# Silu in a hybrid decoder step, written as tanh on ScalarE and a multiply-add on VectorE

## The reference

```python
def swiglu(h, w_gate, w_up, w_down):
    return (jax.nn.silu(h @ w_gate) * (h @ w_up)) @ w_down
...
def decoder_layer(x, pe, mixer, g_ffn1, w1_gate, w1_up, w1_down, g_mix, w_in, w_out,
                  g_ffn2, w2_gate, w2_up, w2_down, g_ple, w_ple_gate, w_ple_proj):
    x = x + 0.5 * swiglu(rms_norm(x, g_ffn1), w1_gate, w1_up, w1_down)
    mixed, state = mixer(rms_norm(x, g_mix) @ w_in)
    x = x + mixed @ w_out
    x = x + 0.5 * swiglu(rms_norm(x, g_ffn2), w2_gate, w2_up, w2_down)
    gate = jax.nn.sigmoid(rms_norm(x, g_ple) @ w_ple_gate)
    x = x + gate * (pe @ w_ple_proj)
    return x, state
```

## Time and profile before

| | |
|---|---|
| median of three runs | 2749.54 us (2747.8 to 2750.54) |
| profiled execution, first to last instruction | 2748.0 us |
| TensorE busy | 2554.6 us, 93% |
| VectorE busy | 1214.8 us, 44% |
| ScalarE busy | 1112.5 us, 40% |
| GpSimd busy | 1006.6 us, 37% |

### The profile page before, as it was taken

How to read it: one execution, slowest core, us unless ns; L and a number is a source line. 1 busy time by engine, 2 the same in 40 slices (tenths; PEclk the granted TensorE clock), 3 DMA queues, 4 the chain that set the end, 5 groups by cost and what they waited for, 6 DMA issues and landing times.

```text
span 2748.0 us, 40635 instructions
## 1 busy us (share of the span) xinstructions
PE 2554.6 (93%) x15166; PEld 2233.7 (81%) x15166; DVE 1214.8 (44%) x3074; ACT 1112.5 (40%) x1833; POOL 1006.6 (37%) x527
## 2 busy tenths in 40 slices
PE   6999999999779988999989988898999999999997
PEld 6999998879657777867876887787889888878787
DVE  4232224628654344443545666565333234322344
ACT  4222223635424343345544544664443233322332
POOL 5333433324434444322542332221224354454340
PEclk9999999999889999999999999999999999999998
DMA  5323323332234454211322221111113222232222
GB/s 173 97 92 106 113 87 111 124 127 95 90 96 145 128 154 136 87 47 54 127 75 73 78 78 47 47 55 39 47 47 115 78 94 90 100 107 94 91 71 73
DMA packets 157030, 253.34 MB, mean 92 GB/s; under 512 B 15009, under 2 KB 101282, under 8 KB 156834
## 3 DMA queue, kind: packets, MB, share of 16 engines
q1 hardware_dynamic: 154144, 247.02, 27.7%
q10 hardware_dynamic: 2690, 3.72, 0.4%
HBM read 240.34 MB, written 18.73 MB: 94 GB/s over the span
## 4 chain that ended last, share of the span: by engine, by line
PE 73%; DVE 11%; ACT 7%; issue 4%; POOL 3%; DVEq 1%; DMA 1%; ACTq 0%; SPq 0%
PE ps L1594 22%; PE ps L1596 21%; PE ps L1595 21%; PE ps L1807 2%; PE ps L1863 2%; POOL w_lo L789 1%; PE ps L1793 1%; PE ps L1729 1%; DVE ps L1159 1%; ACT w_hi L890 1%; DVE ha_lo L1161 1%; POOL kv_kr L839 1%; ACT ha_hi L940 1%; DVE s_hits L1419 1%; DVE xa L1250 1%
## 5 line engine op out<-in xcount | busy, mean ns | idle before, releaser
L789 POOL TENSOR_TENSOR w_lo<-raw,w_hi 128x1024 fp32r<-128x1024 f32 x250 | 599.5, 2400 | 833.2 <-ACT w_hi L890 832.9
L1594 PE MATMUL ps<-xna_hi,w_hi 128*128 128x288 f32 x2000 | 606.6, 303 | 14.1 <-POOL xna_lo L795 7.3
L1595 PE MATMUL ps<-xna_lo,w_hi 128*128 128x288 f32 x2000 | 596.1, 298 | 0.0
L1596 PE MATMUL ps<-xna_hi,w_lo 128*128 128x288 f32 x2000 | 595.6, 298 | 0.0
L789 POOL TENSOR_TENSOR d_lo<-raw,d_hi 128x1024 fp32r<-128x1024 f32 x90 | 214.9, 2388 | 653.0 <-ACT d_hi L890 653.0
L1594 PE MATMUL ps<-xnb_hi,w_hi 128*128 128x512 f32 x1000 | 406.5, 406 | 0.0
L1594 PEld LDWEIGHTS ps<-xna_hi,w_hi 128*128 128x128 f32 x2000 | 382.6, 191 | 27.8 <-issue 17.6
L1596 PE MATMUL ps<-xnb_hi,w_lo 128*128 128x512 f32 x1000 | 394.5, 394 | 0.0
L1595 PE MATMUL ps<-xnb_lo,w_hi 128*128 128x512 f32 x1000 | 393.9, 394 | 0.0
L1595 PEld LDWEIGHTS ps<-xna_lo,w_hi 128*128 128x128 f32 x2000 | 382.4, 191 | 0.2
L1596 PEld LDWEIGHTS ps<-xna_hi,w_lo 128*128 128x128 f32 x2000 | 381.9, 191 | 0.0
(11 more groups left out here) (331 smaller groups left out, 4101.1 us busy)
## 6 DMA issues: line engine op xcount, KB each, us to landing
raw<-in_w_gu SPq DMA_DIRECT2D x176, 512.0 KB, 3.5
raw<-in_w_d SPq DMA_DIRECT2D x88, 512.0 KB, 3.5
raw<-in_w_ring SPq DMA_DIRECT2D x74, 512.0 KB, 3.5
pages<-in_vk_pages SPq DMA_DIRECT2D x256, 128.0 KB, 2.6
idx_flat<-in_idx_pages SPq DMA_DIRECT2D x256, 32.0 KB, 2.4
idxp<-idx_flat SPq DMA_DIRECT2D x8, 1024.0 KB, 6.7
x_spill<-xa SPq DMA_DIRECT2D x1, 2304.0 KB, 8.9
xa<-x_spill SPq DMA_DIRECT2D x4, 576.0 KB, 6.0
```

What stands on the lines that cost most here:

```text
L789: g_.tensor_tensor(lo[slot][:, :, :], raw[l % 2][:, :, :], hi[slot][:, :, :].bitcast(f32), ALU.subtract).then_inc(lo_done, 1)
L1594: mm(out, shi, mhi, start=first, stop=False)
L1595: mm(out, shi, mlo, start=False, stop=False)
L1596: return mm(out, slo, mhi, start=False, stop=last)
```

## The change

silu(z) = z / (1 + exp(-z)) is the same as 0.5 z (1 + tanh(z / 2)). ACT now writes tanh(z / 2) into the tile silu. A new DVE instruction, at the end of the gate product in the list of events (L1157), waits for it, makes (tanh + 1) times z from this tile and the gate's PSUM bank, and writes the tile again. The product with up waits for this, and so does PE ahead of the next use of the gate's bank. What is missing, the factor 0.5, goes into the residual addition: 0.25 where 0.5 was. There are 132 such units: 88 of 288 tokens and 44 of 512.

```diff
@@ ACT, product
                     if j:
                         act.wait_ge(hmul_done, n("unit", f, j - 1, c))
-                    A(silu[g][:, own(c)], z, ACT.Silu).then_inc(silu_done, 1)
+                    A(silu[g][:, own(c)], z, ACT.Tanh, scale=0.5).then_inc(tanh_done, 1)
@@ DVE, product
-                if kind == "up":
+                if kind == "gate":
+
+                    dve.wait_ge(tanh_done, n("unit", *key, c))
+                    v.scalar_tensor_tensor(out=silu[g][:, own(c)], in0=silu[g][:, own(c)], scalar=1.0, in1=z, op0=ALU.add, op1=ALU.mult).then_inc(gated, 1)
+                elif kind == "up":
                     f, j = key
                     u = n("unit", f, j, c)
-                    dve.wait_ge(silu_done, u)
+                    dve.wait_ge(gated, u)
                     dve.wait_ge(prod_done, pn + 1)
@@ DVE, down
-                    v.scalar_tensor_tensor(out=x[g][:, m, own(c)], in0=ps[:, 3 + (i - 1) % 2, 0:CH[c][1]], scalar=0.5,
+                    v.scalar_tensor_tensor(out=x[g][:, m, own(c)], in0=ps[:, 3 + (i - 1) % 2, 0:CH[c][1]], scalar=0.25,
@@ PE, bank_free
                 if kind == "gate":
-                    pe.wait_ge(silu_done, n("unit", *key, c))
+                    pe.wait_ge(gated, n("unit", *key, c))
```

More of the change, by code:

```diff
@@ L593, in program @@
         loaded, hi_done, lo_done = [sem(f"loaded{s}") for s in range(2)], sem("hi_done"), sem("lo_done")
-        prod_done, silu_done, hmul_done, hhi_done, h_ready = sem("prod_done"), sem("silu_done"), sem("hmul_done"), sem("hhi_done"), sem("h_ready")
+        prod_done, tanh_done, gated, hmul_done, hhi_done, h_ready = sem("prod_done"), sem("tanh_done"), sem("gated"), sem("hmul_done"), sem("hhi_done"), sem("h_ready")
         down_done, acc_done = sem("down_done"), sem("acc_done")
```

## The result

The changed kernel takes 2789.24 us (median of four runs, 2786.06 to 2792.03) against 2750.04 before: a ratio of 1.014, with a 95% interval of 1.0126 to 1.0154. It is slower, as forecast, but by 39 us where 11 were forecast, and outside the range.

A forecast was written before the change was run, and what follows sets the result against it. PE was taken as the bound, its idle time set by DVE/ACT search loops. Terms 7.6 + 7.0 - 1.5 - 2 = +11.1 us on 2748.0, with the runs' median 1.5 above, gave 2760.5; forecast 2755 to 2767, range 2744 to 2773.

The forecast's parts named there:

- Which stage bounds, and which wait ends last there: PE, busy 93%, idles mainly beside searches and attention; only its 7% idle time and what lengthens it moves the time.
- The parts and their durations: Whole kernel: 76 loads go, 97.5 us of ACT; 132 DVE instructions of 0.455 or 0.691 us come, 70.4 us.
- Search A, 7.6 us: Search A, 625 to 784 us: new instructions delay DVE's next choice or additions, PE pays in full; loss 7.6 us.
- Search B1, 7.0 us: Search B1, 1555 to 1672 us: eleven gates delay the same search loop, typically 0.75 us each; loss 7.0 us.
- Search B2, a gain of 1.5 us: Search B2 with prompt attention: two loads go around a gate, DVE's wait replaces most; thirteen gates together gain 1.5 us.
- the example's gate: Gate of 1733 us in search B2: choice starts 1.8 us later, some 0.2 of 2.57 us saved on loads arrives.
- sign of being wrong: A search stage no longer than before, or B2 and the sample attention shorter or longer by more than 8 us.
- Rival (c): Slower by more: B2's 1.8 us at each of thirteen gates is not covered; 2784 us, by half 2772; chance 0.12.
- Plain feed-forward stages, 0: Plain feed-forward stages: PE's up product hides the new instruction, with 2.3 us of room at a gate; cost 0.
- Sample attention, a gain of 2 us: Sample attention and the rest: three loads on the chain go, half expected behind PE waits; gain 2 us.
- What the loads are worth: On the chain that ended last, 14 loads of 1.283 us go: 18.0 us at most; by the higher price 37 us.
- Neither theory: Experiments' two explanations of the loss: DVE's in-order wait for the tanh, or the 70 us of added DVE work.

The follow-up runs named there:

- experiment 3: Kernel before, Silu and loads kept, plus only a VectorE wait for the Silu at the gate product's place: 2798.42 us, ratio 1.0163.
- experiment 1: Changed kernel with the multiply-add moved to the up product's place, directly ahead of the product with up: 2760.07 us, ratio 1.0026 to the kernel before.
- experiment 2: Changed kernel without the multiply-add, so the product is tanh times up and a factor is missing: 2747.0 us, ratio 0.9976 to the kernel before.
- experiments 6 and 9: Kernel before with tanh only in search B2 with prompt attention; multiply-add at up's place in the former, 2744.80 us, at the gate's in the latter, 2759.63 us.
- second profiles: The kernel before and the changed kernel, each run once more unchanged and profiled again, to see the scatter; no total time given.
- Experiment 4: Changed kernel with the multiply-add at up's place only in the last feed-forward: 2781.86 us, ratio 1.0106 to the kernel before.
- experiments 4 and 5: Experiment 4, and the kernel before with tanh only in sample attention (multiply-add at the gate) and search B2 (at up): the latter 2744.56 us, ratio 0.9969.
- experiment 10: Kernel before plus a VectorE instruction at each gate's place that leaves its data unchanged and waits for no ScalarE or PE: 2779.23 us, ratio 1.0103.

## Why the prediction was wrong

- *Which stage bounds, and which wait ends last there:* right. PE has idle time mainly beside the searches and the attention, and the loss is there, with one exception below. But that only PE's idle time and what lengthens it counts was too narrow: of the 38 us in the four stages 13 are slower matmuls, which the forecast had at up to 3 us in the range and not in the sum.
- *The parts and their durations:* right. 454 and 688 ns for the new instruction, against 455 and 691 from the earlier trace rows.
- *Search A, 7.6 us:* right, 7.8. At its first gate the tanh and the multiply-add delay the next choice by 2.4 us, forecast 2.47. Of the loss 6.4 us are waits of PE, the rest slower matmuls. The wait alone costs 2.9 us (experiment 3), the multiply-add at up's place 4.9 (experiment 1 against 2).
- *Search B1, 7.0 us:* right in its mechanism, 9.0 measured. The wait alone costs 7.5 us (experiment 3), the multiply-add at up's place 3.1. The sum of the two is 10.6; why it is not 9.0 is not shown.
- *Search B2, a gain of 1.5 us:* this step failed; it lost 10.1. The gain was there: 6.3 us without the multiply-add, 7.1 and 7.7 with a late one. The place at the gate, with its wait, took it back and more, 16.5 us (experiments 6 and 9). The step set the tanh where the load had stood, and did not ask whether PE's gate product had ended by then: at the example's gate it had not. And the clock was put at up to 3 us for all stages, where PE's busy time in this one grew by 7.8. The forecast named as a sign of being wrong that B2 is longer by more than 8 us, and this came. Rival (c) had named the place and 1.8 us for each of thirteen gates, 23.4 us, and got 0.12. That its 2784 lies nearest to the measured time is partly luck: most of B2's loss is at one place and not at thirteen gates, and the last feed-forward was not in it.
- *Plain feed-forward stages, 0:* this step failed for the last one, 10.9 us at one place. The first was at 0, as forecast. The cover was named as the product with up; but behind the new wait on DVE stand also the additions of the preceding down product, for two banks. The zero was worked out at an ordinary gate and carried over to the last stage, where ACT itself waits, for a DMA, ahead of a gate's function. Experiment 4 gives the 10 us back, and experiment 3 makes most of them with a wait alone.
- *Sample attention, a gain of 2 us:* its idle time fell by 2.3 us, as forecast (29.8 to 27.5, and 29.6 to 27.4 in the second profiles). That the stage is not shorter comes from its busy time, 348.4 in both profiles against 341.7 and 346.0. This is not shown to come from the change: the same code was busy 343.3 and 341.5 us in experiments 4 and 5.
- *What the loads are worth:* 18.0 us at most by the forecast, 6.6 measured (experiment 2). That a load lies on the chain that ended last doesn't say that the next wait in line is far behind it. The Trainium skill (ScalarE: Activation LUTs, What ACT_TABLE_LOAD costs) has a price of 2.66 us for every switch to another set. These runs do not show it: each load takes 1283 ns, the Silu behind the one of 666.89 starts 0.02 us after its end, and the 76 that went were worth 6.6 us in all.

Neither theory holds alone. The place of the multiply-add, where DVE waits for the tanh, makes the loss in the last feed-forward and in B2: at up's place the same work loses nothing there. In search A, where DVE is the limit, the work counts for more than the place (4.9 and 3.3 us), in B1 for less (3.1 and 5.7). What stays open is a part of B2's clock: around the example's gate, 1741 to 1781 us of the changed kernel, the matmuls take 3.0 us longer while PE's waits are 0.7 us shorter in sum. Experiments 6 and 9 show that the longer busy time goes with the place, not through what.

## What to carry to other kernels

A wait that is put into an engine's in-order list can be paid by everything behind it, and not only by its own consumer: list what stands behind, for every place where the instruction appears, and above all where the engine waited for is itself waiting, for a DMA or for a matmul. Put an added step next to its consumer if nothing earlier needs it; with the same 132 instructions the change cost 39 us at the gate and 7 us at up. And use a substitution that saves table loads only where loads are really alternating: here on 32 of 132 units, for a gain of 0.3%. And see the shortest and the median beside a mean before an instruction is priced by it: in experiment 10 a mean of 757 ns stood for 458 alone and up to 2602 beside POOL.

## What the runs showed of the hardware

A VectorE instruction that reads fp32 from SBUF by both operands stood until the GpSimd instruction beside it had ended: in experiment 10 all 56 that began while one ran ended 0.31 us (288 columns) or 0.55 us (512) after it or later, and took up to 2.73 us; the other 76 took 436 to 460 and 679 to 694 ns. The operation is the same but for its arithmetic as the multiply-add with one operand from PSUM, which took 442 to 456 and 677 to 691 ns whether GpSimd worked or not. Why the two differ is not shown.

A removed table load made ACT reach its instruction earlier, but at the example's gate in B2 it then stood 1.06 us for PE: a load ahead of a wait is time that may have been idle anyway.
